# Two output projections walked tile by tile, and the last down tile begun one chunk ahead

## The reference

```python
def reference(x, ...):
    for l in range(DEPTH):
        if l % 2 == 0:
            h = _even_mixer(x, even_w_in[j], even_w_out[j], ...)   # ... concatenate([o_a, o_b]) @ w_out
        else:
            h = _odd_mixer(x, fox_w_in[j], fox_w_out[j], ...)      # ... (o * sigmoid(g)) @ w_out
        x = _layer_norm(ALPHA * x + h, ln1_g[l], ln1_b[l])
        x = _layer_norm(ALPHA * x + _swiglu(x, ffn_w1[l], ffn_w2[l]), ln2_g[l], ln2_b[l])
    return x

def _swiglu(x, w1, w2):
    gate, up = jnp.split(x @ w1, 2, axis=-1)
    return (jax.nn.silu(gate) * up) @ w2
```

## Time and profile before

| | |
|---|---|
| three runs | 1400.98, 1402.65 (median), 1405.59 us |
| the profiled execution | 1402.81 us, of which 1401.0 us from first to last instruction |
| TensorE (PE) busy | 1348.9 us, 96%, mean granted clock 0.989 |
| ScalarE (ACT), VectorE (DVE), GpSimd (POOL) busy | 495.6, 474.6, 531.5 us |
| 284 to 345 us, even half's output projection and norm | TensorE busy 56.8 of 61 us |
| 635 to 725 us, first down projection, its norm, start of the odd layer | 85.8 of 90 us |
| 968 to 1048 us, odd half's output projection and norm | 77.1 of 80 us |

### The profile page before, as it was taken

One profiled execution on the slowest core, in us unless ns is written; L12 is line 12 of the kernel. 1 busy time (PEld: TensorE's weight loads), 2 busy tenths in 40 slices (PEclk: granted clock), 3 DMA queues, 4 the chain that ended last, 5 costly groups with the idle time before them and its releaser, 6 DMA issues.

```text
span 1401.0 us, 18949 instructions
## 1 busy us (share of the span) xinstructions
PE 1348.9 (96%) x7304; PEld 1125.0 (80%) x7304; DVE 474.6 (34%) x956; ACT 495.6 (35%) x824; POOL 531.5 (38%) x421
## 2 busy tenths in 40 slices
PE   7998999698999999999999999999999999999997
PEld 7887877588888888888788888877788888888886
DVE  3365435556111111010634555644561111110005
ACT  4313155523322232211255665654333222232111
POOL 5514041232444445544234312222434444445440
PEclk9999999799999999999999999999999999999999
DMA  6311021113333332333133222211223333323221
GB/s 213 110 61 61 31 92 60 61 33 89 91 91 90 104 107 76 120 97 127 25 96 94 66 62 61 61 61 61 91 85 96 90 90 95 108 84 120 91 105 60
DMA packets 141400, 119.60 MB, mean 85 GB/s; under 512 B 5664, under 2 KB 120576, under 8 KB 141312
## 3 DMA queue, kind: packets, MB, share of 16 engines
q1 hardware_dynamic: 141072, 118.10, 27.0%
q10 hardware_dynamic: 240, 0.31, 0.1%
HBM read 116.20 MB, written 2.10 MB: 84 GB/s over the span
## 4 chain that ended last, share of the span: by engine, by line
PE 83%; DVE 7%; ACT 4%; issue 4%; POOL 1%; DMA 0%; ACTq 0%; DVEq 0%; SPq 0%; POOLq 0%
PE banks L507 25%; PE banks L508 25%; PE banks L509 25%; ACT w_hi L1118 1%; PE banks L816 1%; PE banks L974 1%; PE banks L940 1%; PE banks L956 1%; POOL w_lo L1078 1%; PE banks L834 1%; DVE small L1602 1%; DVE xT_lo L1425 1%; PE banks L880 1%; DMA w_raw<-in_even_w_in_dram 0%; DVE x_res L1645 0%
## 5 line engine op out<-in xcount | busy, mean ns | idle before, releaser
L1078 POOL TENSOR_TENSOR w_lo<-w_raw,w_hi 128x512 fp32r<-128x512 f32 x417 | 531.3, 1304 | 838.1 <-ACT w_hi L1118 782.6
L507 PE MATMUL banks<-xT_lo,w_hi 128*128 128x512 f32 (+2 forms) x1024 | 384.3, 375 | 2.5 <-DVEq L1426 2.4
L509 PE MATMUL banks<-xT_hi,w_hi 128*128 128x512 f32 (+2 forms) x1024 | 380.5, 372 | 0.0
L508 PE MATMUL banks<-xT_hi,w_lo 128*128 128x512 f32 (+2 forms) x1024 | 380.4, 372 | 0.0
L1118 ACT ACTIVATE w_hi<-w_raw 128x2048 fp32r<-128x2048 f32 (+1 forms) x107 | 200.0, 1869 | 194.5 <-PE banks L509 151.4
L507 PEld LDWEIGHTS banks<-xT_lo,w_hi 128*128 128x128 f32 (+1 forms) x1024 | 192.2, 188 | 37.4 <-issue 5.1
L509 PEld LDWEIGHTS banks<-xT_hi,w_hi 128*128 128x128 f32 (+1 forms) x1024 | 192.1, 188 | 33.6
L508 PEld LDWEIGHTS banks<-xT_hi,w_lo 128*128 128x128 f32 (+1 forms) x1024 | 192.2, 188 | 32.6
L1675 DVE TENSOR_TENSOR banks<-silu_g,banks 128x512 f32<-128x512 f32 x44 | 30.6, 696 | 403.1 <-PE banks L509 403.1
L507 PE MATMUL banks<-w_lo,xT_hi 128*128 128x256 f32 (+1 forms) x480 | 159.0, 331 | 5.1 <-POOL w_lo L1078 2.8
L508 PE MATMUL banks<-w_hi,xT_lo 128*128 128x256 f32 (+1 forms) x480 | 153.9, 321 | 0.0
(11 more groups left out here) (198 smaller groups left out, 1259.9 us busy)
## 6 DMA issues: line engine op xcount, KB each, us to landing
w_raw<-in_ffn_w_dram SPq DMA_DIRECT2D x92, 512.0 KB, 4.6
w_raw<-in_ffn_w_dram SPq DMA_DIRECT2D x20, 1024.0 KB, 4.9
w_raw<-in_fox_w_in_dram SPq DMA_DIRECT2D x16, 1024.0 KB, 5.8
w_raw<-in_even_w_in_dram SPq DMA_DIRECT2D x14, 1024.0 KB, 5.0
w_raw<-in_even_w_out_dram SPq DMA_DIRECT2D x4, 1024.0 KB, 5.1
w_raw<-in_fox_w_out_dram SPq DMA_DIRECT2D x4, 1024.0 KB, 5.0
x_res<-in_x_dram SPq DMA_DIRECT2D x4, 512.0 KB, 7.9
out_dram<-x_res SPq DMA_DIRECT2D x3, 512.0 KB, 2.6
```

The lines of the kernel that those rows point to most:

```text
L507: mm(acc, l_hi, r_lo, start=first, stop=False)
L508: mm(acc, l_lo, r_hi, start=False, stop=False)
L509: return mm(acc, l_hi, r_hi, start=False, stop=final)
L1078: ins = nc.gpsimd.tensor_tensor(w_lo[c % RING][:, a:a + n], w_raw[c % RAW][:, a:a + n], w_hi[c % RING][:, a:a + n].bitcast(F32), ALU.subtract)
```

## The change

TensorE's program is written in another order at three places; ScalarE's and VectorE's follow at two. In both output projections (`out_tiles`) the products with b (`first(t)`) and those with c2 and d2 (`second(t)`) alternate for tiles 0 and 1; the turns of tiles 0 and 1 stand ahead of and behind the last `first`, ahead of `second(2)`. ScalarE makes the roots and splits of tiles 0 and 1 first, then the rounding of the first up chunk, then the roots of tiles 2 and 3 with the second up chunk's rounding between them. VectorE takes each tile's left half right ahead of its norm, and makes the residual splits of tiles 0 and 1 ahead of the norms of 2 and 3. In the first down projection (`down_tiles`) tile 3's first chunk stands ahead of tile 2's second. The second down projection is as before. The numbers of the banks of some turns change.

```diff
-            def norm_tail(tag, step, src_tiles, lag, early):
-
-                def turn(t):
-
-                    turn_tile(tag, t, x_res, lambda: pe.wait_ge(S["norm_done"], step * NT + t + 1),
-                              4 + 2 * (t % 2))
-
-                for t in range(NT):
-                    src_tiles(t)
-                    if early and t >= lag:
-                        turn(t - lag)
-                if early:
-                    for t in range(NT - lag, NT - 1):
-                        turn(t)
-                    early(0)
-                    turn(NT - 1)
-                    early(1)
-                    turned_tiles[0] += NT
...
+            def turn_normed(tag, step, t, bank):
+                turn_tile(tag, t, x_res, lambda: pe.wait_ge(S["norm_done"], step * NT + t + 1), bank)
...
+                def first(t):
                     pe.wait_ge(S["od_hi"], t + 1)
                     pe.wait_ge(S["od_lo"], t + 1)
                     next(rest)
+
+                src = [(c2, o_hi_e, o_lo_e, 0), (d2, xT_hi, xT_lo, 4)]
+                out_tiles(0, first, src, begun, (6, 2, 4, 6))
...
+            def out_tiles(l, first, src, begun, turn_banks):
+
+                parts = range(len(src))
+
+                def second(t):
+                    if t in begun:
+                        acc_bank[t] = begun[t]
+                        tail_tile((f"out{l}", 1), t, src, parts[1:])
+                        return
+                    open_bank((f"out{l}", 1, "acc", t), (2, 3, 0, 1)[t], "dve")
+                    acc_bank[t] = uses[(f"out{l}", 1, "acc", t)]
+                    tail_tile((f"out{l}", 1), t, src, parts, True)
+
+                def turn(t):
+                    turn_normed(f"n1_{l}", 2 * l, t, turn_banks[t])
+
+                first(0)
+                second(0)
+                first(1)
+                second(1)
+                first(2)
+                turn(0)
+                first(3)
+                turn(1)
+                second(2)
+                second(3)
                 gemm_banks[0], gid[0] = 4, 2
-                src = [(c2, o_hi_e, o_lo_e, 0), (d2, xT_hi, xT_lo, 4)]
-                tail_products(("out0", 1), src, "n1_0", 0, 2, lambda i: up_product(0, i, 0), begun=begun,
-                              places=(2, 3, 0, 1))
+                turn(2)
+                up_product(l, 0, 0)
+                turn(3)
+                up_product(l, 1, 0)
+                turned_tiles[0] += NT
...
-                drain(rest)
-                src = [(c2, o_hi4, o_lo4, 0), (d2, xT_hi, xT_lo, 4)]
-                tail_products(("out1", 1), src, "n1_1", 2, 2, lambda i: up_product(1, i, 0))
-
-            def tail_products(name, parts, tag, step, lag, early, acc_open=False, begun={}, places=None):
-                def tile(t):
-                    key = (*name, t)
-                    if t in begun:
-                        acc_bank[t] = begun[t]
-                    elif not acc_open:
-                        open_bank((*name, "acc", t), places[t] if places else next_gemm_bank(), "dve")
-                        acc_bank[t] = uses[(*name, "acc", t)]
-                    acc = psum[acc_bank[t][0]][:, :]
-                    tok = slice(t * P, (t + 1) * P)
-                    for n, (c, src_hi, src_lo, k0) in enumerate(parts):
-                        if n == 0 and t in begun:
-                            continue
-                        if t == 0:
-                            weights_in(c)
-                        nk = chunks[c][2] // 512
-                        for k in range(nk):
-                            ins = products(acc, src_hi[:, k0 + k, tok], src_lo[:, k0 + k, tok],
-                                           hi(c, k * 512, 512), lo(c, k * 512, 512),
-                                           not acc_open and n == 0 and k == 0,
-                                           n == len(parts) - 1 and k == nk - 1)
+
+                out_tiles(1, first, [(c2, o_hi4, o_lo4, 0), (d2, xT_hi, xT_lo, 4)], {}, (4, 2, 6, 4))
...
+            def tail_tile(name, t, parts, which, start=False):
+
+                key = (*name, t)
+                acc = psum[acc_bank[t][0]][:, :]
+                tok = slice(t * P, (t + 1) * P)
+                for n in which:
+                    c, src_hi, src_lo, k0 = parts[n]
+                    if t == 0:
+                        weights_in(c)
+                    nk = chunks[c][2] // 512
+                    for k in range(nk):
+                        ins = products(acc, src_hi[:, k0 + k, tok], src_lo[:, k0 + k, tok],
+                                       hi(c, k * 512, 512), lo(c, k * 512, 512),
+                                       start and n == 0 and k == 0, n == len(parts) - 1 and k == nk - 1)
+                    if n == len(parts) - 1:
+                        uses[key] = acc_bank[t]
+                        close_bank(key, ins)
                         if t == NT - 1:
-                            if n < len(parts) - 1:
-                                used_alone(c, ins)
-                            else:
-                                uses[key] = acc_bank[t]
-                                close_bank(key, ins)
-                                used_with_bank(c, key)
-                        elif n == len(parts) - 1:
-                            uses[key] = acc_bank[t]
-                            close_bank(key, ins)
-
-                norm_tail(tag, step, tile, lag, early)
+                            used_with_bank(c, key)
+                    elif t == NT - 1:
+                        used_alone(c, ins)
+
+            def down_tiles(l, parts):
+
+                tile = lambda t, which: tail_tile((f"down{l}", 1), t, parts, which)
+                if l == 1:
+                    for t in range(NT):
+                        tile(t, range(3))
+                    return
+
+                def turn(t):
+                    turn_normed("n2_0", 1, t, 4 + 2 * (t % 2))
+
+                tile(0, range(3))
+                tile(1, range(3))
+                turn(0)
+                tile(2, (0,))
+                tile(3, (0,))
+                tile(2, (1, 2))
+                turn(1)
+                tile(3, (1, 2))
+                turn(2)
+                fox_start(0)
+                turn(3)
+                fox_start(1)
+                turned_tiles[0] += NT
...
-                hi_upto(stage_chunks[f"out{l}"][0] + 3)
-                hi_upto(stage_chunks[f"out{l}"][2] + 2)
-                hi_upto(stage_chunks[f"up{l}"][0] + 1)
-                norm_act(f"n1_{l}", 2 * l, stage_chunks[f"up{l}"][0], 2)
-
-            def norm_act(tag, step_n, after, lag=1):
+                hi_upto(stage_chunks[f"out{l}"][3] + 1)
+                tag, up = f"n1_{l}", stage_chunks[f"up{l}"][0]
+                nc.scalar.preload_act_table_set(LN_EXP)
+                ln_root(2 * l, 0)
+                ln_root(2 * l, 1)
+                split_hi(tag, 0)
+                split_hi(tag, 1)
+                hi_upto(up + 1)
+                ln_root(2 * l, 2)
+                hi_upto(up + 2)
+                ln_root(2 * l, 3)
+                split_hi(tag, 2)
+                split_hi(tag, 3)
+                hi_upto(up + 3)
...
-                for t in range(NT):
-                    add_left((f"out{l}", 0, t), t, 0)
-                norm(f"n1_{l}", (f"out{l}",), 2 * l)
+                tag, name = f"n1_{l}", (f"out{l}",)
+                add_left((*name, 0, 0), 0, 0)
+                norm_tile(tag, name, 2 * l, 0)
+                add_left((*name, 0, 1), 1, 0)
+                norm_tile(tag, name, 2 * l, 1)
+                split_lo(tag, 0)
+                add_left((*name, 0, 2), 2, 0)
+                split_lo(tag, 1)
+                add_left((*name, 0, 3), 3, 0)
+                norm_tile(tag, name, 2 * l, 2)
+                norm_tile(tag, name, 2 * l, 3)
+                split_lo(tag, 2)
+                split_lo(tag, 3)
```

More of the change, by code:

```diff
@@ L749, in swiglu @@
                     k0 += chunks[cs[i]][2] // 512
-                tail_products((f"down{l}", 1), parts, f"n2_{l}", 2 * l + 1, 1,
-                              fox_start if l == 0 else None, acc_open=True)
+                down_tiles(l, parts)
             running = {}
@@ new lines, in norm_tile @@
+            def norm_tile(tag, name, n, t):
+                add_left((*name, 1, t), t, 1)
+                st = stats[:, t, :]
+                chain(v.bn_aggr(st[:, 12:14], st[:, 0:12]), S["ln_arg"])
+                dve.wait_ge(rows_in[n // 2], 32 * (n % 2 + 1))
+                gain, bias = (norm_rows[n][:, i, :] for i in range(2))
+                xs = x_res[:, t, :]
+                step(stt(xs, xs, st[:, 12:13], gain, ALU.subtract, ALU.mult))
+                dve.wait_ge(S["ln_done"], n * NT + t + 1)
+                r, tmp = st[:, 14:15], st[:, 15:16]
+                step(stt(tmp, st[:, 13:14], 1e-5, r, ALU.add, ALU.mult))
+                step(stt(tmp, tmp, -0.5, r, ALU.mult, ALU.mult))
```

(13 more changed lines are left out.)

35 lines of the change are left out of this document (6 added, 29 removed).

## The result

| | before | changed |
|---|---|---|
| timed side by side, four runs each | median 1401.98 us (1400.98 to 1405.59) | 1416.61 us (1415.57 to 1417.23) |
| ratio, 95% interval | | 1.0098 (1.0083 to 1.0112) |
| the profiled execution | 1402.81 us, span 1401.0 | 1415.57 us, span 1413.8 |

The change makes the kernel about 1% slower. Times of one kernel spread by some 5 us: of the 60 runs of the kernel before that were timed beside the experiments, those with a mean granted clock of 0.988 or 0.989 took 1400.4 to 1403.4 us and those with 0.984 to 0.987 took 1403.0 to 1406.2 us. The busy times of the page after answer to the earlier trace rows: TensorE has 5.1 us more of busy time with the same 7304 products, and the other engines hardly more.

What follows compares the result with a forecast made beforehand. TensorE's fixed work plus its holes was taken as the bound. From the profiled execution's time, 1402.8 - 0.8 (even half) + 2.6 (down projection) + 7.8 (odd half) = 1412.4 us, range 1407 to 1417.

Steps and rivals of the forecast that it cites:

- Even half, -0.8 us: Even half's output projection: old waits go, a 3.0 us wait for d2's split comes; 0.8 us gained (3.1 gained to 1.8 lost).
- The clock's 1.5 us: Even half: loss to low clock behind the new wait for d2's split, 1.5 us (bounds nothing and 3 us).
- The 0.8 us for the norm of tile 2: Both halves: tile 2's turn waits 0.8 us for its norm, through one 1.1 us collision with GpSimd's split (even-half bounds 0 and 1.9).
- Down projection, +2.6 us: First down projection: foxq0's rounding and split move later with tile 2's statistics, TensorE waits until 699.3; 2.6 us lost.
- the bound of 6: Down projection: upper bound of the loss, 6 us, if the low clock lasts as long as around 255 us.
- Odd half, +7.8 us: Odd half's output projection: TensorE waits 6.4 us for c2, losing three b tiles' cover; 7.8 us lost (bounds 6.0 and 10.6).
- the 1.0 us of clock behind d2: Odd half: loss to low clock after d2's products start at 1007.9, put at 1.0 us (bounds 0 and 2.7).
- The rule weighed: Odd half: bursts shorter than operand waits start at half rate; tile 0's parts at 1.2 GHz, clock loss 2.7 us, not 1.0.
- The cheap down place: Rival: down projection costs nothing if foxq0's rounding is let through ahead; 1409.8 us, chance 0.06.
- The dear clock: Rival: low clock lasts 10.3 us from restart; odd half 1.7 more, down projection 3.4 more, 1417.5 us, chance 0.08.
- The faster case: Rival: c2 and d2 splits arrive ahead of tile 0, old end holes go; 1398.2 us, chance 0.04.

Runs made afterwards that it cites:

- the three undone parts: Changed kernel with one place each back in its old order: odd half 1405.16 us, down projection 1408.95 us, even half 1411.81 us.
- the second timing: The changed kernel timed again with nothing altered: 1413.61 us, ratio to before 1.0077.
- the kernel that lets it through: Changed kernel, but in the down projection ScalarE rounds the next stage's first chunk ahead of the root of tile 2: 1410.14 us, ratio to before 1.0040.
- the kernel with both repairs: Changed kernel with the next chunk rounded earlier in the down projection, c2 and d2 rounded earlier and two b tiles ahead in the odd half: 1400.76 us, ratio 0.9984.
- the early rounding: Down projection's next chunk rounded ahead of tile 2's root: on the changed kernel 1410.14 us; on before with only the even half changed 1405.97 us.
- the odd half undone: Changed kernel with the odd half's order of tiles, turns, roundings and norms as before: 1405.16 us, ratio to before 1.0014.
- the down projection undone: Changed kernel with only the first down projection back in its old order: 1408.95 us, ratio to before 1.0040.

## Why the prediction was right, point by point

The forecast, slower through three new or longer waits for GpSimd's splits, is what happened: the three undone parts give back what the traces show at their places. 1416.6 us lies inside the range, 4.2 above the number, but above the forecast's own spread (1408 to 1415.5), in the part of the range that was there for a dearer clock. The rise was written as 9.6 us; it measured 14.6 at the medians, 10.6 at the second timing, and 11.5 over the three places of the first trace. The other 1.3 us of that trace lie ahead of 294 us and are no effect of the change. The terms:

- **Even half, -0.8 us.** Sign right. The wait at d2 is 2.78 us where I had 3.0. The clock's 1.5 us are a matter of chance: paid in five executions of this order (-0.2 to -0.3 us) and not in six (-1.8 to -1.9), mine lying between them. The 0.8 us for the norm of tile 2 did not come; GpSimd's burst stretched that tile's first step by 0.5 us only (1.78 against 1.28), and 0.58 us came at tile 3 instead. Up0 starts at 328.85 us, 1.3 of which were lost ahead of 294 us.
- **Down projection, +2.6 us.** The mechanism is right and the size is not. ScalarE's rounding moved to 691.52 with the root of tile 2 and the split of tile 1, as written, and GpSimd starts at 693.51. But the wait grew by 3.33 us, not 2.6. GpSimd's fourth piece ended 5.9 us after the first began, in place of 5.0 before. It took 2.24 us in place of 1.27, beside VectorE's scaling of tile 3 and the one-column step behind it (2.02 and 1.10 us). In before, the fourth piece lay beside the same scaling too and was not stretched; VectorE's operation was (2.36 us). And I left the clock's loss as it was, which is the term that was mis-sized: with the same wait of 5.7 us the place came to between +3.4 and +4.0 us five times, with 2.8 to 4.2 us of low clock behind the wait, and to between +6.1 and +6.4 three times, with 5.5 to 6.2 us of it and a second stretch of 3.4 us between 722 and 728 us. In those three the bound of 6 was passed.
- **Odd half, +7.8 us.** It measured 6.9 to 7.3 in all six executions with this order. The wait is 6.28 us (6.4 written), c2's 12 products take 4.93 us, most of it at 1.2 GHz (5.1 written), and d2 starts 14.23 us behind the first product with b, against 14.39 before: the 36 uncovered products are the cost, as the step said. The low clock over c2 cost nothing by itself, for GpSimd ended d2's split only at 1013.40 us. Too much were the 1.0 us of clock behind d2 and the 0.8 us for the norm of tile 2: the windows are at full clock from 1015 us on, and the turn of tile 2 waited for nothing. That would leave 6.0 us; counted from the first product with b, up1 starts 6.3 us later than before, and another 0.7 us came behind it, 0.56 of them in a wait for the norm of tile 3 that the step did not have.
- **The rule weighed.** The Trainium skill, "TensorE: Matmul & The Clock Gate", section "HAM oscillation — how this bites in real kernels", would have both parts of tile 0 at half rate. The c2 part was. By the time of the d2 part the clock was back (granted 1.00 from 1015 us on), and no second wait had opened between them. The trace agrees with half of it.
- **The rivals.** The cheap down place is excluded as it stands, since the rounding is not let through ahead; but the kernel that lets it through shows that it was the better half of the idea. The dear clock did not come as written, with 10.3 us of low level from the restart (6.0 us at the down projection, 4.3 in the odd half), but at the down projection its size did, through the second stretch: 3.0 us more than the longer wait explains, where the rival had 3.4. The faster case was to decide below 4.6 us of waits; they came to 12 us more than before, and the kernel with both repairs, where only the 2.76 us are left, is not slower than before by any reading.

## What to carry to other kernels

When an order of products is changed to free a buffer or finish a tile sooner, look at what feeds it: the two engines that prepare the operand must be in the new order too, or the place that was gained is a place to wait. Compare the time at which each operand is ready with the time at which its first reader now stands there; behind one tile of 2.7 us, a split of 5 us that starts with it is late by the difference or more (2.78 us here). And an edit's worth may have the opposite sign without its partner: the early rounding gave 4.9 to 7.9 us with the new order and lost 1.7 to 3.2 with the old one.

## What the runs showed of the hardware

- **The low clock behind a hole is not the same in each execution.** Behind the same wait of 2.8 us in the same order, the window of 300 to 306 us had a granted clock of 1.00 in six executions and 0.72 to 0.74 in five, even in two whose first marks lay 0.01 us apart (the odd half undone, and the down projection undone). Behind the hole of 2.39 us it was 0.50 at 697.2 to 700.6 us in before's trace and 1.00 at 699 to 702 us in the one with the down projection undone. A hole of 1.8 us near 720 us stands in all fourteen traces, and the clock fell behind it in four. The stretch behind the 2.8 us costs some 1.6 us: the even half is at -0.2 to -0.3 us with it and at -1.8 to -1.9 without. The four timings of the kernel before gave medians from 1401.98 to 1404.67 us; the mean granted clock of its runs goes with this, the part of the 5 us of spread ahead of 294 us is not shown.
- **GpSimd's burst and VectorE's operations stretch each other.** GpSimd's four pieces took 5.04 us at 294.93 us in before and 5.9 beside the norm, where one of them took 2.24 us in place of 1.27. Of the norms' steps with 1024 columns, none of the fourteen traces has one over 1.29 us without a GpSimd operation beside it; with one, some took 1.5 to 2.4 us, and a step on a single column up to 1.22 us, in place of 0.16. Which of the two engines is held up differs: in before VectorE's operation was (2.36 us, the piece 1.27), in the changed kernel both were. The pairing is read from the timelines; no run separated the two engines.
